# Second attention: denominators applied to the output, weight splits on VectorE, modulation pieces a block later

## The reference

```python
# layer 0 (tokens and a context of 256 tokens, 512 columns together)
m0 = split(silu(c) @ w_mod[0] + b_mod[0], 6);  hl = modulate(rms_norm(xl), m0[0], m0[1])
u = hl @ w_pw1; a, gate = split(u, 2); u = a * sigmoid(gate)
u = depthwise_conv(u, w_dw, 31 taps) + b_dw          # over the tokens
u = silu(layer_norm(u)) @ w_pw2;  xl = xl + m0[2] * u
xl = xl + m0[5] * (relu(hl' @ w_ff1[0]) ** 2 @ w_ff2[0])
# layer 1: 16 query heads of 64, 4 key heads; 256 queries look at 512 keys (context and tokens)
m1 = split(silu(c) @ w_mod[1] + b_mod[1], 6)          # w_mod[1] is 1024 x 6144
q, k, v = rms_norm and rotary of (hl @ w_qkv)
s = q @ k.T / 8;  p = softmax(s);  o = p @ v          # second attention
xl = xl + m1[2] * (o @ w_o);  xl = xl + m1[5] * (relu(hl' @ w_ff1[1]) ** 2 @ w_ff2[1])
```

## Time and profile before

| what | us |
|---|---|
| time, median of 3 runs | 1544.14 (1543.37 to 1545.25) |
| profiled execution, its time | 1544.38 |
| profiled execution, its span | 1542.5 |
| PE busy | 1457.6 (94%) |
| DVE busy | 749.0 (49%) |
| ACT busy | 614.5 (40%) |
| POOL busy | 406.1 (26%) |

### The profile page before, as it was taken

How to read it: one execution, slowest core, us unless ns; L and a number is a source line. 1 busy time by engine, 2 the same in 40 slices (tenths; PEclk the granted TensorE clock), 3 DMA queues, 4 the chain that set the end, 5 groups by cost and what they waited for, 6 DMA issues and landing times.

```text
span 1542.5 us, 25177 instructions
## 1 busy us (share of the span) xinstructions
PE 1457.6 (94%) x10880; PEld 1253.0 (81%) x10880; DVE 749.0 (49%) x921; ACT 614.5 (40%) x753; POOL 406.1 (26%) x324
## 2 busy tenths in 40 slices
PE   5799999988999997999799999999999989899999
PEld 5688889988999995765276888888886855799999
DVE  7975645365545466567654121212124577443343
ACT  4433364434333456121345222322224447544443
POOL 4977712100002410000000232343230020134553
PEclk9899999999999998999899999999999989999999
DMA  7466676544655564886434323222233310345552
GB/s 256 164 219 211 221 240 219 203 160 137 191 179 178 189 219 159 265 239 189 151 109 166 108 84 106 87 105 98 93 109 110 101 64 1 110 137 191 172 184 82
DMA packets 158259, 239.37 MB, mean 155 GB/s; under 512 B 5680, under 2 KB 128592, under 8 KB 158032
## 3 DMA queue, kind: packets, MB, share of 16 engines
q1 hardware_dynamic: 153360, 232.85, 45.4%
q10 hardware_dynamic: 4800, 5.08, 1.4%
HBM read 227.55 MB, written 1.05 MB: 148 GB/s over the span
## 4 chain that ended last, share of the span: by engine, by line
PE 84%; DVE 7%; ACT 6%; issue 2%; DMA 1%; POOL 0%; DVEq 0%; SPq 0%; ACTq 0%; POOLq 0%
PE bank L1968 24%; PE bank L1969 24%; PE bank L1970 24%; PE bank L2036 2%; PE bank L2273 2%; ACT A L589 1%; DVE wlo L1085 1%; ACT whi L633 1%; ACT ahi L593 1%; PE bank L2433 1%; PE bank L2110 1%; DVE stat L1713 1%; PE bank L563 1%; PE bank L544 1%; PE bank L2145 1%
## 5 line engine op out<-in xcount | busy, mean ns | idle before, releaser
L1968 PE MATMUL bank<-ahi,whi 128*128 128x256 f32 (+1 forms) x2480 | 792.7, 320 | 38.5 <-DVE wlo L1085 10.3
L1969 PE MATMUL bank<-alo,whi 128*128 128x256 f32 (+1 forms) x2480 | 784.1, 316 | 0.0
L1970 PE MATMUL bank<-ahi,wlo 128*128 128x256 f32 (+1 forms) x2480 | 783.4, 316 | 0.0
L1085 DVE TENSOR_TENSOR wlo<-raw,whi 128x2048 fp32r<-128x2048 f32 x158 | 362.2, 2292 | 533.1 <-ACT whi L633 533.0
L633 ACT ACTIVATE whi<-raw 128x2048 fp32r<-128x2048 f32 x160 | 306.3, 1914 | 726.2 <-PE bank L1970 726.2
L1968 PEld LDWEIGHTS bank<-ahi,whi 128*128 128x128 f32 x2480 | 477.8, 193 | 85.9 <-issue 40.9
L1970 PEld LDWEIGHTS bank<-ahi,wlo 128*128 128x128 f32 x2480 | 477.9, 193 | 28.8
L1969 PEld LDWEIGHTS bank<-alo,whi 128*128 128x128 f32 x2480 | 478.2, 193 | 27.8 <-issue 0.2
L1906 POOL TENSOR_TENSOR alo<-A,ahi 128x512 fp32r<-128x512 f32 (+1 forms) x43 | 125.8, 2927 | 351.8 <-ACT ahi L833 351.8
L1924 POOL TENSOR_TENSOR A<-A 128x512 f32 (+1 forms) x48 | 96.6, 2025 | 442.7 <-ACT A L956 442.7
L1560 DVE SCALAR_TENSOR_TENSOR A<-A,decay 128x512 f32<-128x512 f32 x80 | 53.8, 749 | 0.0
(11 more groups left out here) (302 smaller groups left out, 1200.8 us busy)
## 6 DMA issues: line engine op xcount, KB each, us to landing
raw<-in_w_ff SPq DMA_DIRECT2D x64, 1024.0 KB, 5.2
A<-in_w_mod SPq DMA_DIRECT2D x60, 512.0 KB, 4.7
raw<-in_w_in SPq DMA_DIRECT2D x28, 1024.0 KB, 8.2
modraw<-in_w_mod SPq DMA_DIRECT2D x36, 512.0 KB, 4.8
raw<-in_pw SPq DMA_DIRECT2D x12, 1024.0 KB, 8.4
raw<-in_w_ffn_gate SPq DMA_DIRECT2D x11, 1024.0 KB, 5.3
raw<-in_w_ffn_up SPq DMA_DIRECT2D x11, 1024.0 KB, 5.3
raw<-in_w_ffn_down SPq DMA_DIRECT2D x11, 1024.0 KB, 4.9
```

The source lines that it names most:

```text
L1085: dve.tensor_tensor(wlo[:, k % 2, :], raw[:, (k + 2) % 4, :], whi[:, k % 2, :].bitcast(F32), ALU.subtract).then_inc(wlo_ready, 1)
L1968: pe.matmul(out_, w_hi, a_hi, start=start, stop=False, **kw)
L1969: pe.matmul(out_, w_hi, a_lo, start=False, stop=False, **kw)
L1970: return pe.matmul(out_, w_lo, a_hi, start=False, stop=stop, **kw)
```

## The change

It has three parts.

1. **Second attention.** The probabilities are no longer scaled. TensorE weighs v with the raw exponentials, and two more products per step (a column of reciprocals, spread to 64 columns, times the identity) put the reciprocals of the denominators beside the output in the same bank. ScalarE copies this spread to SBUF (`gspread`), VectorE multiplies the output with it (`gnorm`), ScalarE makes the high half (`gout`), VectorE the low half (`glo`). From step 4 on, VectorE copies bank 5 of the turned probabilities (`gptb`) and ScalarE only bank 4. The turn now waits for the exponentials, no longer for VectorE's scaling; the weighing waits for the reciprocals.
2. **Weight splits.** GpSimd no longer splits the first two blocks of `w_o`. VectorE does, one in round 17 and one at the end of the attention, and ScalarE's rounded copy of the second block stands in round 10.
3. **Convolution stage.** Each pair of pieces from 8 on comes one block later on TensorE; those from 22 on are spread over the end of the stage in another way; on ScalarE `mod_rows` comes behind the split of the same block. SyncE's list is unchanged.

```diff
@@ area @@
+        spd = area(13824, 256)
+        onorm = area(14080, 256)
@@ ScalarE, pw1 @@
+                ahead(p)
                 if p.least in (0, 4):
                     mod_rows(1, p.least // 4)
-                ahead(p)
@@ ScalarE, second attention @@
-                for s in range(2):
-                    c = act.activation(ptg[:, i % 2, 512 * s:512 * s + 512], pb[4 + s][:, :], ACT.Copy)
-                c.then_inc(pt_ready, 1)
+                if i < 4:
+                    act.activation(ptg[:, i % 2, 512:1024], pb[5][:, :], ACT.Copy).then_inc(pt_ready, 1)
+                act.activation(ptg[:, i % 2, 0:512], pb[4][:, :], ACT.Copy).then_inc(pt_ready, 1)
+
+            def gspread(c):
+                act.wait_ge(o_done, TR + 2 * c + 2)
...
+                act.activation(spd, pb[6 + c % 2][:, 256:512], ACT.Copy).then_inc(ohi_ready, 1)
 
             def gout(c):
-                act.wait_ge(o_done, TR + 2 * c + 2)
-                act.activation(ahi[:, 256 * c:256 * c + 256], pb[6 + c % 2][:, 0:256], ACT.Copy).then_inc(ohi_ready, 1)
+                act.wait_ge(olo_ready, TR + 2 * c + 1)
+                act.activation(ahi[:, 256 * c:256 * c + 256], onorm, ACT.Copy).then_inc(ohi_ready, 1)
...
                 if i >= 5 and i % 2:
-                    gout((i - 5) // 2)
+                    gspread((i - 5) // 2)
+                if i >= 6 and i % 2 == 0:
+                    gout((i - 6) // 2)
                 if 0 <= i - 2 < GSTEPS:
                     gpt(i - 2)
-            ahead(Pos(FIRST["qkv"] + 5, 5))
+                if i == 10:
+                    ahead(Pos(FIRST["qkv"] + 5, 5))
@@ VectorE, second attention @@
-            def gscale(i):
...
-                link(dve.reciprocal(stat[:, s1:s1 + 2], stat[:, s0:s0 + 2]))
-                for b in range(2):
-                    m = dve.tensor_scalar(pg[:, i % 2, b, :], pg[:, i % 2, b, :], stat[:, s1 + b:s1 + b + 1],
-                                          None, ALU.mult)
+            def ginvert(i):
...
+                dve.reciprocal(stat[:, s1:s1 + 2], stat[:, s0:s0 + 2]).then_inc(pn_ready, 1)
+
+            def gptb(i):
+                dve.wait_ge(pt_done, TR + i + 1)
+                dve.wait_ge(o_done, TR + i - 1)
+                dve.tensor_copy(ptg[:, i % 2, 512:1024], pb[5][:, :]).then_inc(pt_ready, 1)
+
+            def gnorm(c):
+                dve.wait_ge(ohi_ready, TR + 2 * c + 1)
...
+                dve.tensor_tensor(onorm, pb[6 + c % 2][:, 0:256], spd, ALU.mult).then_inc(olo_ready, 1)
...
+                if i == GSTEPS + 1:
+                    ahead(Pos(FIRST["qkv"] + 4, 4))
+            ahead(Pos(FIRST["qkv"] + 5, 5))
@@ GpSimd @@
-            split_ahead(4)
-            split_ahead(5)
@@ TensorE, pw1 @@
                 if l == 0:
                     mod_pieces(4, 4)
-                mod_pieces(8 + 2 * l, 2)
+                else:
+                    mod_pieces(6 + 2 * l, 2)
             convolve(4)
...
@@ TensorE, second attention @@
             def gturn(i):
-                pe.wait_ge(pn_ready, TR + i + 1)
+                pe.wait_ge(exp_done, TR + 2 * (i + 1))
...
             def gweigh(i):
...
+                pe.wait_ge(pn_ready, TR + i + 1)
...
+                for b in range(2):
+                    pe.matmul(pb[6 + c % 2][64 * b:64 * b + 64, 256 + P * qt:256 + P * qt + P],
+                              stat[:, s1 + b:s1 + b + 1].broadcast_to([P, 64]), C["ident"], start=True, stop=True)
+                pe.wait_ge(pt_ready, TR + 2 * (i + 1))
```

More of the change, by code:

```diff
@@ L1744, in _ @@
                 if 0 <= i - 2 < GSTEPS:
-                    gscale(i - 2)
+                    ginvert(i - 2)
+                    if i - 2 >= 4:
+                        gptb(i - 2)
+                if i >= 6 and i % 2 == 0:
+                    glo((i - 6) // 2)
                 if i >= 5 and i % 2:
-                    glo((i - 5) // 2)
+                    gnorm((i - 5) // 2)
+                if i == GSTEPS + 1:
+                    ahead(Pos(FIRST["qkv"] + 4, 4))
+            ahead(Pos(FIRST["qkv"] + 5, 5))
             ph[0] = "wo"
-            dve.wait_ge(wlo_ready, FIRST["wo"] + 2)
             for l in range(4):
@@ L2296, in _ @@
             convolve(5)
-            for c in range(2, 4):
+            for c in range(2, 5):
                 channel_sum(c)
+            mod_pieces(22, 2)
+            channel_sum(5)
+            mod_pieces(24, 2)
             convolve(6)
             mod_turn(1, 2)
-            mod_pieces(24, 2)
             convolve(7)
-            channel_sum(4)
-            channel_sum(5)
+            channel_sum(6)
             mod_pieces(26, 2)
-            channel_sum(6)
             channel_sum(7).then_inc(msum_done, 1)
-            mod_pieces(28, 2)
             for u in range(KD):
@@ L2311, in _ @@
                 quad_sums(pe, pb[2][:, 0:128], csq[:, u % 4, :], 128, u == 0, u == KD - 1).then_inc(vsum_done, 1)
+            mod_pieces(28, 2)
             pe.wait_ge(lrstd_ready, 1)
@@ L2470, in _ @@
                     gweigh(i - 3)
-            pe.wait_ge(olo_ready, TR + 8)
+            pe.wait_ge(olo_ready, TR + 16)
             for l in range(4):
```

29 lines of the change are left out of this document (14 added, 15 removed).

## The result

| what | before | after |
|---|---|---|
| time, median of 20 runs each | 1544.81 (1543.15 to 1547.70) | 1547.36 (1544.51 to 1549.96) |
| ratio of after to before, with its 95% interval | | 1.0013 (1.0007 to 1.0019) |
| profiled execution, its span | 1542.5 | 1545.6 |

The changed kernel is some 2 to 2.5 us slower, where 4 us less had been forecast. The direction was wrong, and the time lies 2.9 us above the range. By the bound of 0.2% it is no change that this measurement can tell for certain, though the interval lies wholly above 1.

The account below looks back on a forecast made before the run. TensorE was taken to bound the kernel, with 84% of the chain, so edits count by the waits they remove. Stage -0.3 and attention -3.7 made -4.0 us, so 1540.1 us against a 1544.81 median; range 1535 to 1544.5.

Parts of the forecast that it names:

- Start of pw1: TensorE's 5.91 us wait at the start of the convolution stage goes; block 1 ends at 622.7, 8.8 us earlier.
- Shift 2: SyncE's copies behind 2 MB of loads stall TensorE 0.7 us (between 0 and 2) ahead of `convolve(4)`, which starts at 715.0.
- Pieces 22 and 23, and SyncE's start: End of the convolution stage: these pieces run at 728.7 on TensorE, SyncE's copies of shift 3 start at 730.2.
- Landing of shift 3: SyncE's eight copies land so that `convolve(6)` begins at 739.7, against 739.34 before; bounds 737.7 and 743.3.
- Rival (a): SyncE's half of shift 3 takes 13.1 us: +3.6, sum -0.4, 1543.7; chance 0.16.
- Behind the wait: From `convolve(6)` to the last sum: 12.3 us plus 2.1 for half clock, ending at 754.1, 0.3 earlier than before.
- The whole 8.8 us waited away in one place, 7.9 us long: The gain from the start of pw1 is lost in TensorE's wait for SyncE's copies ahead of `convolve(6)`.
- Attention: Second attention: first rounds gain 8.2 us, 3.61 us steps lose 3.8, the end loses 0.7; -3.7 us in all.
- (b): No ring in the attention: ScalarE's and VectorE's extra pair hides, TensorE sets the step; -2.5, 1537.6; chance 0.11.
- (d): Granted clock falls in the attention's loop, 2.4 us a spell; three spells make 1547.3; chance 0.07.
- (e): Attention's turn still waits, for ScalarE's copies; first rounds gain 5.3, not 8.2; sum -1.1, 1543.0; chance 0.10.
- Rival (c): `convolve(6)` does not need SyncE's half so late and starts 7.9 us earlier: 10.0 less, 1530.1; chance 0.08.

Follow-up runs that it names:

- The experiment with 1 MB ahead: Convolution stage's part alone, but in shift 2 the 1 MB load for pw2 behind SyncE's copies, against the kernel before: 0.9996 (0.9987 to 1.0005).
- the copies first: SyncE's shift copies issued ahead of the loads of pieces, against the kernel before: 0.9927 with the stage's part alone, 0.9896 with the whole change.
- the attention alone: The change's norms and weight splits on VectorE, with the convolution stage of before, against the kernel before: 0.9986 (0.9977 to 0.9995), 2.2 us faster.

## Why the prediction was wrong

**Start of pw1: right.** Block 1 follows without a wait and ends at 622.09 (forecast 622.7).

**Shift 2: the step that failed first.** The prediction took the 2 MB of loads as 5 us of DMA time and 5.8 us for issuing the copies, and a stall between 0 and 2 us, of which 0.7. It was 3.56, outside these bounds, which did not enter the range of the stage either. The 5.8 us were the time to issue eight copies, not to land them: eight need 7.8 us with nothing ahead (measured in shift 3), and 14.6 behind 2 MB. It also left out what the wait does to the clock: `convolve(4)` lost 2.85 us more. Together 5.7 us. The experiment with 1 MB ahead shows the size of this one term: 5.0 us of the time (1549.74 to 1544.70). The kernel is then within 0.6 us of before, near the stage's -0.3, but by luck in part: its wait ahead of `convolve(6)` was 9.96 us, not 7.9.

**Pieces 22 and 23, and SyncE's start: mechanism right, times late by the first miss.** Forecast 728.7 and 730.2, measured 733.82 and 735.44.

**Landing of shift 3: mis-sized.** The sum had 9.5 us from the first copy to `convolve(6)`; it was 11.9. Of the 2.4 us, 1.6 are the halving: half of the 12.3 us of the earlier trace rows is 6.2, and eight copies with nothing ahead took 7.8, near the 7.5 of the prediction's own lower bound, which had been worked out from the issuing. The rest is the loads ahead, which cost 4.1 us here and 3.25 in the sum (3.65 less the 0.4 between load and first copy). The Trainium skill's interleaving (DMA: Bandwidth & Descriptors, "Issuing engines are not separate DMA queues") was quoted against 13.1 us for the half; the 7.8 us agree. It is no statement on loads ahead from the same engine, and these were what was missing. Rival (a), 13.1 us, had the right sign and the wrong cause: the copies alone are not slow. By both misses `convolve(6)` began 7.6 us later than forecast (747.30, not 739.7).

**Behind the wait: right.** From `convolve(6)` to the end of the last sum 14.1 us (to 761.4), forecast 14.4; the spread took 1.16, the 0.9 gain that the prediction named and did not count.

**The whole 8.8 us waited away in one place, 7.9 us long: half right.** The gain was waited away and more, but in two places, 3.56 and 10.35 us. The chain that the prediction gave for the second (pieces used late, loads issued late, copies behind them) is what the copies first took away.

**Attention: right up to `w_o`, the size with some luck.** Counted from the first exponentials, the forecast had step 3 at 10.9, step 6 at 22.5 and step 15 at 55.3; measured 10.66, 22.13 and 55.06. The steps were 3.61 to 3.65 apart, and 3.93 at the one with ScalarE's weight copy (forecast 3.91). The end took 8.53 us (forecast 8.3). At `w_o` 3.76 us were gained (forecast 3.7). But both numbers are against one trace of before, and most other traces of that attention are 0.6 us or more shorter; the ratio of the attention alone says 2.2 us, with the clock behind `w_o`'s wait in it. What the sum lacked is the 1.4 us of clock behind the 2.75 us wait there. Rivals (b), (d) and (e) did not come: no step near 3.36 from step 6 on, no fall of the clock in the loop, and the turn waited for ScalarE's copy without losing the first rounds' gain.

**Rival (c)**, the front gain stays, was given 0.08. Its condition did not hold: `convolve(6)` needs SyncE's half. But the gain stays once the copies do not stand behind loads: with the whole change, then, the time is 1528.1, near its 1530.1.

## What to carry over

When work is moved to a later place on one engine, the loads that refill its buffers move too, and with them everything that stands behind these loads in the issuing engine's list; here a small urgent copy belonged ahead of large loads that nobody needed soon. An urgent DMA is to be priced by its landing behind the bytes already issued, not by the time to issue it. And a wait of TensorE like those here, from 2.75 us up, is to be priced with a possible spell of half clock behind it, 0 to 2.9 us on top, even where one trace shows none.

## What the runs showed of the hardware

- Eight copies of 142 KB from SBUF to SBUF, issued by one engine, took 7.8 us from the first issue to the convolution that needs them (one trace); behind 1 MB of loads from the same engine 11.5 to 12.8, behind 2 MB 14.6 to 14.8. Taking away the loads issued behind them changed nothing clear of the spread (11.8).
- Sixteen such copies from two engines, started together, took 13.1 to 13.5 us in seven traces; so half of them takes not half the time.
- What the granted clock does after a wait of TensorE is not settled by the length of the wait. Behind 3.48 to 3.86 us the convolution lost nothing in three traces (3.49, 3.49, 3.58), 1.7 us in three (3.60, 3.72, 3.86), and 2.7 to 2.9 in six (3.48, 3.50, 3.56, 3.71, 3.73, 3.74). The attention alone gave 0 and 1.7 in its two profiles. After 0.70 nothing was lost, after 5.85 it was 2.1, after 9.96 and 11.30 2.8, after 10.29 and 10.35 it was 1.5 to 1.6.
- A split of 4.6 us on GpSimd held up a product of VectorE from 0.69 to 4.32 us, and one of 4.7 us the two scalings of the earlier trace rows from 0.88 to 6.17.
